# Two of the four weight sums of a seven-product pair, by accumulating DMAs from GpSimd

## The chip, the cores and the metric

One core of a Trainium2 chip runs the whole program. The metric is the device time of one execution in microseconds (us). The kernel before has a median of 1961.26 us in 3 runs (1959.46 to 1963.83).

## The reference

Two layers of a decoder trunk on 512 tokens of width 1024, with 16 learned tokens put in front (528 in all). Each layer has a gated feed-forward network, a mixer (pooling and gated linear attention side by side) and a second feed-forward network, each with a residual and a layer norm:

```python
def swiglu(x, w_gate, w_up, w_down):
    return (jax.nn.silu(x @ w_gate) * (x @ w_up)) @ w_down
...
    for l in range(DEPTH):
        h = layer_norm(a * h + 0.5 * swiglu(h, ffn1_w_gate[l], ffn1_w_up[l], ffn1_w_down[l]),
                       ln1_g[l], ln1_b[l])
        z = h @ w_in[l]
        ...
        h = layer_norm(a * h + y, ln2_g[l], ln2_b[l])
        h = layer_norm(a * h + 0.5 * swiglu(h, ffn2_w_gate[l], ffn2_w_up[l], ffn2_w_down[l]),
                       ln3_g[l], ln3_b[l])
    return h[:, N_META:]
```

All of it is float32, with d_ff = 2816, which is 22 tiles of 128. The change touches the gate and up products of the four feed-forward networks alone.

## The kernel before

**Precision.** A float32 operand is split into a high part (rounded to fp32r by ACT) and a low part (operand minus high part, by DVE or POOL). A product is three matmuls: high x high, high x low, low x high. So every weight block needs a `hi` and a `lo` before PE can use it.

**Stream of weights.** The weights lie in HBM as pieces of [128 x 1024] floats (512 KB), in the order of use. SP loads piece n into `raw[:, n % 2, :]` as soon as piece n-2 has been split (`wait_piece`, the loop at L314 to L316). ACT makes `w_hi` (`high_part`, L852), and POOL (`split`, L330) or, in the fast part, DVE (`raw_low`, L1195) makes `w_lo`, four slots of each.

**The fast part.** A network goes through the 22 tiles of d_ff in three phases of 8, 8 and 6. In a phase the gate and up pieces of each tile m come first, then 8 pieces of the down matrix. Tiles 0 to 3 are computed classically. For tiles 4 to 21 (18 in each network, 72 in all) the gate and up products together, taken over two halves of the tokens and two halves of the inner dimension, are a 2x2 block product. It is done with 7 block products in place of 8 (`fast_pair`, L430 and on): 7 x 4 x 3 = 84 matmuls of 128x264. Three of the seven use blocks of the weights as they lie in `raw`. Four use sums of weight blocks:

```python
s_sum[0] = u[low] + u[high]
s_sum[2] = g[low] + u[low]
s_sum[1] = s_sum[0] + g[low]
s_sum[3] = s_sum[1] + g[high]
```

where g and u are the gate and the up piece and low and high are their halves of 512 columns (`w_sums`, from L1172). ACT makes `s_hi` of each (`sum_high`, L846), DVE `s_lo` (`sum_low`, L1200). Sums of token blocks (`v_hi`, `v_lo`) are made once per network.

**The order of work** on every engine is written out by hand. While PE does pair i, DVE runs one iteration of the loop in `ffn` (L1237 to L1263): the four sums of pair i+1, `prod` of the tile before (L1129), `w_lo` of pair i+1 (L1195, twice), `s_lo` 1, `h_lo` (L1134), PS + `p_copy` (L1252), `s_lo` 2 and 3, PS + `u_copy` (L1259), `s_lo` 4. PE's last product of pair i needs the first of these two PSUM sums (`c22_done`). ACT does in the same time a copy of PSUM, `silu`, `w_hi` of the next pair, two copies, and the four `s_hi`. POOL does nothing in this part. It splits the classic pieces, the pieces of the down matrix and those of the mixer. At the end of a phase DVE adds the down product to X, piece by piece, and makes the sums of the next phase's first pair between pieces 4 and 5.

`s_lo_done`, `s_sum_done` and the like count instructions of one kind; 4*i+j stands for sum j of pair i.

## Time and profile before

| | us |
|---|---|
| median of 3 runs | 1961.26 |
| profiled execution, its own time | 1958.71 |
| its span | 1957.0 |
| PE matmul busy | 1886.8 |
| PE weight loads busy | 1802.3 |
| DVE busy | 1232.3 |
| ACT busy | 825.4 |
| POOL busy | 446.2 |

The busy time of an engine is the time in which at least one of its instructions ran. Matmuls overlap in the pipeline, so their mean durations (some 284 ns) are longer than the distance between two (some 121 ns). "Idle before" a group, with the releaser behind the arrow, tells what ended the waits of its instructions. The chain of work that ended last is 86% PE and 9% DVE.

### The profile page before, as it was taken

Reading aid. Unit: us, or ns where it says so; the run is one execution under the profiler, and the core shown is the slowest. Engines: PE = TensorE matmul, PEld = TensorE weight load, DVE = VectorE, ACT = ScalarE, POOL = GpSimd, SP = SyncE. Lnnn points to the kernel's source line nnn. Section 1 sums busy time; section 2 is a strip of 40 time slices with the busy share of each in tenths; the row PEclk is TensorE's granted clock in tenths of the full one; section 3 lists DMA queues with packets and bytes.
Section 4 is the critical chain, followed back from the end, with each engine's and each line's share of the span. In section 5 each row is a group of like instructions: output and inputs, shape, how many; then the busy total and the mean of one; then the engine's idle time right before and its main releaser. Section 6 shows DMA issues by size and latency. Waiting matters only on the chain.

```text
span 1957.0 us, 34609 instructions
## 1 busy us (share of the span) xinstructions
PE 1886.8 (96%) x14406; PEld 1802.3 (92%) x14406; DVE 1232.3 (63%) x1834; ACT 825.4 (42%) x1297; POOL 446.2 (23%) x200
## 2 busy tenths in 40 slices
PE   8999999989999999999999999999899999999996
PEld 8999999879898999999999999998797778899895
DVE  6728557667448837728487385577674488386475
ACT  4525435452125534525455254354431255345253
POOL 4030302332122240030521203023321221402113
PEclk9999999989898999999989999999898889999998
DMA  4333323321111332233323233232211113333232
GB/s 152 100 103 106 104 91 104 97 66 55 44 48 50 102 104 97 92 101 106 114 75 100 95 108 109 87 109 87 65 55 44 54 53 99 108 108 109 86 110 86
DMA packets 48828, 175.26 MB, mean 90 GB/s; under 512 B 5408, under 2 KB 5408, under 8 KB 48672
## 3 DMA queue, kind: packets, MB, share of 16 engines
q1 hardware_dynamic: 48240, 171.78, 28.0%
q8 instruction: 115, 1.88, 0.4%
q10 hardware_dynamic: 432, 1.25, 0.2%
q14 instruction: 41, 0.34, 0.1%
HBM read 170.92 MB, written 2.10 MB: 88 GB/s over the span
## 4 chain that ended last, share of the span: by engine, by line
PE 86%; DVE 9%; issue 2%; ACT 2%; DMA 1%; POOL 0%; DVEq 0%; ACTq 0%
PE PS L371 13%; PE PS L372 13%; PE PS L373 13%; PE PS L424 12%; PE PS L427 12%; PE PS L426 12%; PE PS L403 2%; PE PS L381 2%; PE PS L382 1%; PE PS L679 1%; PE PS L712 1%; DVE win L1533 1%; PE PS L524 1%; PE PS L710 1%; DVE qt L1488 1%
## 5 line engine op out<-in xcount | busy, mean ns | idle before, releaser
L330 POOL TENSOR_TENSOR w_lo<-raw,w_hi 128x1024 fp32r<-128x1024 f32 x172 | 431.3, 2511 | 1483.4 <-ACT w_hi L852 1058.8
L371 PE MATMUL PS<-h_hi,w_hi 128*128 128x264 f32 (+1 forms) x1238 | 370.2, 299 | 0.5 <-DVE h_lo L1134 0.2
L372 PE MATMUL PS<-h_lo,w_hi 128*128 128x264 f32 (+1 forms) x1238 | 369.7, 299 | 0.0
L373 PE MATMUL PS<-h_hi,w_lo 128*128 128x264 f32 (+1 forms) x1238 | 369.4, 298 | 0.0
L852 ACT ACTIVATE w_hi<-raw 128x1024 fp32r<-128x1024 f32 x240 | 215.1, 930 | 231.8 <-PE PS L373 179.1
L424 PE MATMUL PS<-v_hi,s_hi 128*128 128x264 f32 (+1 forms) x864 | 245.0, 284 | 6.1 <-DVE s_lo L1200 6.1
L371 PE MATMUL PS<-x_hi,w_hi 128*128 128x264 f32 (+2 forms) x796 | 245.2, 308 | 5.0 <-DVE ft L1526 4.9
L426 PE MATMUL PS<-v_lo,s_hi 128*128 128x264 f32 (+1 forms) x864 | 244.3, 283 | 0.0
L427 PE MATMUL PS<-v_hi,s_lo 128*128 128x264 f32 (+1 forms) x864 | 243.9, 282 | 0.0
L372 PE MATMUL PS<-x_lo,w_hi 128*128 128x264 f32 (+2 forms) x796 | 242.2, 304 | 0.0
L371 PEld LDWEIGHTS PS<-h_hi,w_hi 128*128 128x128 f32 x1238 | 233.0, 188 | 9.1 <-DVE h_lo L1134 1.6
L373 PE MATMUL PS<-x_hi,w_lo 128*128 128x264 f32 (+2 forms) x796 | 241.2, 303 | 0.0
L372 PEld LDWEIGHTS PS<-h_lo,w_hi 128*128 128x128 f32 x1238 | 233.1, 188 | 7.4
L373 PEld LDWEIGHTS PS<-h_hi,w_lo 128*128 128x128 f32 x1238 | 232.3, 188 | 7.3
L846 ACT ACTIVATE s_hi<-s_sum 128x512 fp32r<-128x512 f32 x288 | 177.5, 630 | 98.3 <-PE PS L427 96.8
L1200 DVE TENSOR_TENSOR s_lo<-s_sum,s_hi 128x512 fp32r<-128x512 f32 x288 | 190.1, 685 | 18.4 <-ACT s_hi L846 18.2
L424 PEld LDWEIGHTS PS<-v_hi,s_hi 128*128 128x128 f32 x864 | 162.5, 188 | 6.8 <-issue 6.8
L371 PEld LDWEIGHTS PS<-x_hi,w_hi 128*128 128x128 f32 x796 | 154.7, 194 | 12.9 <-issue 7.6
L427 PE MATMUL PS<-x_hi,w_lo 128*128 128x264 f32 (+1 forms) x576 | 163.0, 283 | 0.0
L426 PEld LDWEIGHTS PS<-v_lo,s_hi 128*128 128x128 f32 x864 | 162.9, 189 | 0.0
L424 PE MATMUL PS<-x_hi,w_hi 128*128 128x264 f32 (+1 forms) x576 | 162.7, 282 | 0.0
L427 PEld LDWEIGHTS PS<-v_hi,s_lo 128*128 128x128 f32 x864 | 162.4, 188 | 0.0
(217 smaller groups left out, 4008.2 us busy)
## 6 DMA issues: line engine op xcount, KB each, us to landing
raw<-in_stream SPq DMA_DIRECT2D x316, 512.0 KB, 3.7
raw_first<-in_stream SPq DMA_DIRECT2D x4, 512.0 KB, 5.7
out_t<-X SPq DMA_DIRECT2D x8, 256.0 KB, 2.1
X<-in_x_t SPq DMA_DIRECT2D x7, 264.0 KB, 7.5
par<-in_params ACTq DMA_DIRECT2D x2, 480.0 KB, 3.6
X<-in_x_t ACTq DMA_DIRECT2D x1, 264.0 KB, 4.5
```

The source lines that it names most:

```text
L330: nc.gpsimd.tensor_tensor(w_lo[:, slot, :], raw[:, slot % RAWS, :], w_hi[:, slot, :].bitcast(F32), ALU.subtract).then_inc(lo_done[slot], 1)
L371: nc.tensor.matmul(o, hi, rhs_hi[:, k, tok], start=first, stop=False)
L372: nc.tensor.matmul(o, hi, rhs_lo[:, k, tok], start=False, stop=False)
L373: return nc.tensor.matmul(o, lo, rhs_hi[:, k, tok], start=False, stop=last)
L381: nc.tensor.matmul(o, hi[j], x_hi[:, k, tok], start=k == 0, stop=False)
L403: m = nc.tensor.matmul(o, hi[j], x_lo[:, k, tok], start=False, stop=k == KC - 1)
L424: nc.tensor.matmul(o, hi[:, w], rhs_hi[:, k, :], start=start and k == 0, stop=False, skip_group_check=True)
L426: nc.tensor.matmul(o, hi[:, w], rhs_lo[:, k, :], start=False, stop=False, skip_group_check=True)
L427: m = nc.tensor.matmul(o, lo[:, w], rhs_hi[:, k, :], start=False, stop=stop and k == BAND - 1, skip_group_check=True)
L846: nc.scalar.activation(s_hi[:, j - 1, :], s_sum[:, j - 1, :], ACT.Copy).then_inc(S["s_hi_done"], 1)
L852: nc.scalar.activation(w_hi[:, n % SLOTS, part], raw[:, n % RAWS, part], ACT.Copy).then_inc(S["raw_hi"], 1)
L1200: V.tensor_tensor(s_lo[:, j - 1, :], s_sum[:, j - 1, :], s_hi[:, j - 1, :].bitcast(F32), ALU.subtract).then_inc(S["s_lo_done"], 1)
```

## The change

Two sums, 1 and 3, share the block u[low]. SP now loads this block twice into a new buffer `s_two` (one DMA with a broadcast source, 512 KB into two halves), double-buffered over pairs (`load_shared`). POOL waits for the landing and issues two accumulating DMAs of 256 KB each (`add_other`), which add u[high] to the one copy and g[low] to the other, straight from HBM. DVE keeps two adds, for sums 2 and 4, into a single buffer `s_more`. The up piece's load into `raw` brings only its upper half, as nothing else reads the lower one. ACT's and DVE's waits follow; at the first pair of a network they also wait for `v_lo`, because the new buffers share memory with `v_sum`. A first pair's DMAs stand two pieces earlier in the queues of SP and POOL.

```diff
--- before.py
+++ after.py
@@ -75,7 +75,6 @@
 BAND = 4
 BLOCK = BAND * P
 FAST = MT - CLASSIC
-S_ORDER = (1, 3, 2, 4)
 V_ORDER = (3, 1, 2, 4)
 
 
@@ -115,6 +114,13 @@
         if at <= r < at + 2 * nm:
             return m0 + (r - at) // 2 < CLASSIC
     return True
+
+
+FAST_GATES = {gate_piece(l, f, m) - 1: fast_index(l, f, m)
+              for l in range(DEPTH) for f in range(2) for m in range(CLASSIC, MT)}
+PHASE_FIRST = {fast_index(l, f, max(m0, CLASSIC)) for l in range(DEPTH) for f in range(2) for m0, _ in PHASES}
+
+SUMS_BEFORE = {max(n - 2, SLOTS + RAWS) if i in PHASE_FIRST else n: (i, n) for n, i in FAST_GATES.items()}
 
 
 def stream_ready(l, idx):
@@ -189,7 +195,7 @@
         warm = sb("warm", [P, 2])
         rms_eps = sb("rms_eps", [P, 1])
         with ExitStack() as s6:
-            s_sum = sb("s_sum", [P, 4, BLOCK], F32, s6)
+            s_two = sb("s_two", [P, 2, 2, BLOCK], F32, s6)
         acc_a = sb("acc_a", [P, HEADS, NCH, CH])
         acc_t = sb("acc_t", [META, HEADS, META])
 
@@ -207,6 +213,8 @@
         with ExitStack() as s5:
             s_hi = sb("s_hi", [P, 4, BLOCK], F32R, s5)
             s_lo = sb("s_lo", [P, 4, BLOCK], F32R, s5)
+            sb("reserve_v_sum", [P, 4 * BAND * HALF - 8 * BLOCK], F32, s5)
+            s_more = sb("s_more", [P, 2, BLOCK], F32, s5)
         with ExitStack() as s2:
             ex = sb("ex", [P, 4, T], F32, s2)
             kt = sb("kt", [P, 2, 2, T], F32, s2)
@@ -285,6 +293,8 @@
         x_loaded = [sem(f"x_loaded{k}") for k in range(KC)]
         first_full = [sem(f"first_full{i}") for i in range(SLOTS)]
         raw_full = [sem(f"raw_full{i}") for i in range(RAWS)]
+        s_loaded = [sem(f"s_loaded{i}") for i in range(2)]
+        s_added = [sem(f"s_added{i}") for i in range(2)]
         lo_done = [sem(f"lo_done{i}") for i in range(SLOTS)]
         block = ctx.enter_context(nc.Block())
 
@@ -296,6 +306,17 @@
 
         def wait_raw(eng, n):
             eng.wait_ge(raw_full[n % RAWS], 16 * ((n - SLOTS) // RAWS + 1))
+
+        def wait_added(eng, i):
+            eng.wait_ge(s_added[i % 2], 32 * (i // 2 + 1))
+
+        def two_term(i, j):
+
+            return s_two[:, i % 2, j // 2, :]
+
+        def summed_weights(i, j):
+
+            return two_term(i, j) if j % 2 else s_more[:, j // 2 - 1, :]
 
         def wait_stream(eng, l, idx):
             name, value = stream_ready(l, idx)
@@ -311,9 +332,23 @@
                     sp.dma_start(X[:, n, :], x_t[n * P:(n + 1) * P, :]).then_inc(x_loaded[n], 16)
             for n in range(RAWS):
                 sp.dma_start(raw[:, n, :], stream[SLOTS // RAWS, n]).then_inc(raw_full[n], 16)
+
+            def load_shared(i, gate):
+
+                if i > 0:
+                    sp.wait_ge(S["s_lo_done"], 4 * max(i - 1, 1))
+                if i % FAST < 2 and i >= FAST:
+                    sp.wait_ge(S["o_acc"], 4 * ((i // FAST + 1) // 2))
+                shared = stream[(gate + 1) // RAWS, (gate + 1) % RAWS][:, 0:BLOCK]
+                sp.dma_start(s_two[:, i % 2, :, :], shared.rearrange("p (o c) -> p o c", o=1)
+                             .to_broadcast([P, 2, BLOCK])).then_inc(s_loaded[i % 2], 16)
+
             for n in range(SLOTS + RAWS, DEPTH * LAYER_PIECES):
+                if n in SUMS_BEFORE:
+                    load_shared(*SUMS_BEFORE[n])
                 wait_piece(sp, n - RAWS)
-                sp.dma_start(raw[:, n % RAWS, :], stream[n // RAWS, n % RAWS]).then_inc(raw_full[n % RAWS], 16)
+                part = slice(BLOCK if n - 1 in FAST_GATES else 0, PIECE)
+                sp.dma_start(raw[:, n % RAWS, part], stream[n // RAWS, n % RAWS][:, part]).then_inc(raw_full[n % RAWS], 16)
 
             for k in range(KC):
                 sp.wait_ge(S["x_full_done"], DEPTH * LN_PER * KC - KC + k + 1)
@@ -352,7 +387,17 @@
                 n += 1
                 pool.wait_ge(S["consts"], n)
             nc.gpsimd.memset(acc_t[:, :, :], 0.0).then_inc(S["masks"], 1)
+
+            def add_other(i, gate):
+
+                pool.wait_ge(s_loaded[i % 2], 16 * (i // 2 + 1))
+                for j, n, part in ((1, gate + 1, slice(BLOCK, PIECE)), (3, gate, slice(0, BLOCK))):
+                    pool.dma_start(two_term(i, j), stream[n // RAWS, n % RAWS][:, part],
+                                   accum_op=ALU.add).then_inc(s_added[i % 2], 16)
+
             for n in range(SLOTS, DEPTH * LAYER_PIECES):
+                if n in SUMS_BEFORE:
+                    add_other(*SUMS_BEFORE[n])
                 if whole(n):
                     split(n)
             pool.wait_ge(S["mean_first_copied"], DEPTH * LN_PER)
@@ -840,10 +885,15 @@
 
             def sum_high(i, j):
 
-                act.wait_ge(S["s_sum_done"], 4 * i + S_ORDER.index(j) + 1)
+                if j % 2:
+                    wait_added(act, i)
+                else:
+                    act.wait_ge(S["s_sum_done"], 2 * i + j // 2)
                 if i > 0:
                     act.wait_ge(S[("p5_acc", "p6_acc", "p7_acc", "p3_acc")[j - 1]], i)
-                nc.scalar.activation(s_hi[:, j - 1, :], s_sum[:, j - 1, :], ACT.Copy).then_inc(S["s_hi_done"], 1)
+                if i % FAST == 0:
+                    act.wait_ge(S["v_lo_done"], 4 * (i // FAST) + 4)
+                nc.scalar.activation(s_hi[:, j - 1, :], summed_weights(i, j), ACT.Copy).then_inc(S["s_hi_done"], 1)
 
             def high_part(n, part):
 
@@ -1169,26 +1219,18 @@
                 V.tensor_tensor(v_lo[:, j - 1, :, 0:n], v_sum[:, j - 1, :, 0:n], v_hi[:, j - 1, :, 0:n].bitcast(F32),
                                 ALU.subtract).then_inc(S["v_lo_done"], 1)
 
-            def w_sums(i, gate, js):
-
-                low, high = slice(0, BLOCK), slice(BLOCK, 2 * BLOCK)
-                g, u = raw[:, gate % RAWS, :], raw[:, (gate + 1) % RAWS, :]
-                for j in js:
-                    if i > 0:
-                        dve.wait_ge(S["s_lo_done"], 4 * (i - 1) + j)
-                    if j == 1:
-                        wait_raw(dve, gate + 1)
-                        x = V.tensor_tensor(s_sum[:, 0, :], u[:, low], u[:, high], ALU.add)
-                    elif j == 3:
-                        wait_raw(dve, gate)
-                        x = V.tensor_tensor(s_sum[:, 2, :], g[:, low], u[:, low], ALU.add)
-                    elif j == 2:
-                        dve.wait_ge(S["s_sum_done"], 4 * i + 1)
-                        x = V.tensor_tensor(s_sum[:, 1, :], s_sum[:, 0, :], g[:, low], ALU.add)
-                    else:
-                        dve.wait_ge(S["s_sum_done"], 4 * i + 3)
-                        x = V.tensor_tensor(s_sum[:, 3, :], s_sum[:, 1, :], g[:, high], ALU.add)
-                    x.then_inc(S["s_sum_done"], 1)
+            def w_sums(i, gate):
+
+                g = raw[:, gate % RAWS, :]
+                wait_added(dve, i)
+                wait_raw(dve, gate)
+                if i > 0:
+                    dve.wait_ge(S["s_lo_done"], 4 * i)
+                if i % FAST == 0:
+                    dve.wait_ge(S["v_lo_done"], 4 * (i // FAST) + 4)
+                V.tensor_tensor(s_more[:, 0, :], two_term(i, 1), g[:, 0:BLOCK], ALU.add).then_inc(S["s_sum_done"], 1)
+                dve.wait_ge(S["s_sum_done"], 2 * i + 1)
+                V.tensor_tensor(s_more[:, 1, :], s_more[:, 0, :], g[:, BLOCK:PIECE], ALU.add).then_inc(S["s_sum_done"], 1)
 
             def raw_low(n, part):
                 dve.wait_ge(S["raw_hi"], n + 1)
@@ -1197,7 +1239,7 @@
 
             def sum_low(i, j):
                 dve.wait_ge(S["s_hi_done"], 4 * i + j)
-                V.tensor_tensor(s_lo[:, j - 1, :], s_sum[:, j - 1, :], s_hi[:, j - 1, :].bitcast(F32),
+                V.tensor_tensor(s_lo[:, j - 1, :], summed_weights(i, j), s_hi[:, j - 1, :].bitcast(F32),
                                 ALU.subtract).then_inc(S["s_lo_done"], 1)
 
             def pair_low(gate):
@@ -1228,7 +1270,7 @@
                                 v_low(l, f, span, 3)
                                 v_low(l, f, span, 4)
                             if m == CLASSIC - 2:
-                                w_sums(fast_index(l, f, CLASSIC), gate + 4, S_ORDER)
+                                w_sums(fast_index(l, f, CLASSIC), gate + 4)
                                 pair_low(gate + 4)
                             if m == CLASSIC - 1:
                                 for j in range(1, 5):
@@ -1239,7 +1281,7 @@
                         after_fast = m > m0 and m > CLASSIC
                         ps = 2 * (m % 2)
                         if follows:
-                            w_sums(i + 1, gate + 2, S_ORDER)
+                            w_sums(i + 1, gate + 2)
                         if after_fast:
                             fast_prod(l, f, m - 1, F22, span)
                         if follows:
@@ -1283,10 +1325,8 @@
                             dve.wait_ge(S["down_evac"], l * 32 + 16 * f + 8)
                             V.tensor_tensor(halves(X[:, mo, :], span), halves(X[:, mo, :], span), pair(mo % 4, span),
                                             ALU.add).then_inc(S["down_evac"], 1)
-                        if mo == 4:
-                            w_sums(i, nxt, S_ORDER[0:2])
-                        elif mo == 5:
-                            w_sums(i, nxt, S_ORDER[2:4])
+                        if mo == 5:
+                            w_sums(i, nxt)
                         elif mo == 6:
                             pair_low(nxt)
                             sum_low(i, 1)
```

On SP, before, every entry of the stream is one load of a piece that waits for the piece two before it (rows from the first pair's gate piece on; lo_done is the count of a slot's split pieces):

```order
L316 DMA raw<-in_stream 128x1024 [waits lo_done2]
L316 DMA raw<-in_stream 128x1024 [waits lo_done3]
L316 DMA raw<-in_stream 128x1024 [waits lo_done0]
L316 DMA raw<-in_stream 128x1024 [waits lo_done1]
L316 DMA raw<-in_stream 128x1024 [waits lo_done2]
```

Now, at the same place (again from the first pair's gate piece on), with `s_two` for the shared block:

```order
L351 DMA raw<-in_stream 128x1024 [waits lo_done2]
L351 DMA raw<-in_stream 128x512 [waits lo_done3]
L343 DMA s_two<-in_stream 128x2x512 [waits s_lo_done]
L351 DMA raw<-in_stream 128x1024 [waits lo_done0]
L351 DMA raw<-in_stream 128x512 [waits lo_done1]
L343 DMA s_two<-in_stream 128x2x512 [waits s_lo_done]
L351 DMA raw<-in_stream 128x1024 [waits lo_done2]
L351 DMA raw<-in_stream 128x512 [waits lo_done3]
L343 DMA s_two<-in_stream 128x2x512 [waits s_lo_done]
L351 DMA raw<-in_stream 128x1024 [waits lo_done0]
```

A load of `s_two` has come before each pair's gate piece, with a wait of its own on `s_lo_done`, and the up piece's load is half as wide.

On DVE, before, one steady iteration of the pair loop (names: PS is PSUM, p_copy and u_copy copies of it in SBUF):

```order
L1181 TENSOR_TENSOR s_sum<-raw 128x512
L1184 TENSOR_TENSOR s_sum<-raw 128x512
L1187 TENSOR_TENSOR s_sum<-s_sum,raw 128x512
L1190 TENSOR_TENSOR s_sum<-s_sum,raw 128x512
L1129 SCALAR_TENSOR_TENSOR prod<-PS,silu 128x528
L1195 TENSOR_TENSOR w_lo<-raw,w_hi 128x1024
L1195 TENSOR_TENSOR w_lo<-raw,w_hi 128x512
L1200 TENSOR_TENSOR s_lo<-s_sum,s_hi 128x512
L1134 TENSOR_TENSOR h_lo<-prod,h_hi 128x528
L1252 TENSOR_TENSOR PS<-PS,p_copy 128x264
L1200 TENSOR_TENSOR s_lo<-s_sum,s_hi 128x512 x2
L1259 TENSOR_TENSOR PS<-PS,u_copy 128x264
```

Now:

```order
L1231 TENSOR_TENSOR s_more<-s_two,raw 128x512
L1233 TENSOR_TENSOR s_more<-s_more,raw 128x512
L1179 SCALAR_TENSOR_TENSOR prod<-PS,silu 128x528
L1237 TENSOR_TENSOR w_lo<-raw,w_hi 128x1024
L1237 TENSOR_TENSOR w_lo<-raw,w_hi 128x512
L1242 TENSOR_TENSOR s_lo<-s_two,s_hi 128x512
L1184 TENSOR_TENSOR h_lo<-prod,h_hi 128x528
L1294 TENSOR_TENSOR PS<-PS,p_copy 128x264
L1242 TENSOR_TENSOR s_lo<-s_more,s_hi 128x512
L1242 TENSOR_TENSOR s_lo<-s_two,s_hi 128x512
L1301 TENSOR_TENSOR PS<-PS,u_copy 128x264
```

The adds that read `raw` alone are gone, and the two that are left follow each other.

On POOL, before, the whole program behind its constants:

```order
L350 AFFINE_SELECT level_mask<-level_mask 128x64
L354 MEMSET acc_t 16x64
L330 TENSOR_TENSOR w_lo<-raw,w_hi 128x1024 x172
L361 TENSOR_TENSOR X<-X,mean 128x512 x4
```

Now, from the first pieces on to the first down pieces:

```order
L365 TENSOR_TENSOR w_lo<-raw,w_hi 128x1024 [waits raw_hi] x2
L395 DMA s_two<-in_stream 128x512 [waits s_loaded0]
L395 DMA s_two<-in_stream 128x512
L365 TENSOR_TENSOR w_lo<-raw,w_hi 128x1024 [waits raw_hi] x2
L395 DMA s_two<-in_stream 128x512 [waits s_loaded1]
L395 DMA s_two<-in_stream 128x512
L395 DMA s_two<-in_stream 128x512 [waits s_loaded0]
L395 DMA s_two<-in_stream 128x512
L395 DMA s_two<-in_stream 128x512 [waits s_loaded1]
L395 DMA s_two<-in_stream 128x512
L365 TENSOR_TENSOR w_lo<-raw,w_hi 128x1024 [waits raw_hi] x6
```

Pairs of DMAs stand between the subtractions, each pair behind a wait for SP's load.

## Rows read from the trace of the kernel before

**Rows 1.** engines and granted clock, from the page

```profile
PE 1886.8 (96%) x14406; PEld 1802.3 (92%) x14406; DVE 1232.3 (63%) x1834; ACT 825.4 (42%) x1297; POOL 446.2 (23%) x200
...
PEclk9999999989898999999989999999898889999998
```

**Rows 2.** windows inside runs of pairs (us, busy (instructions) by engine, clock, DMA share, GB/s)

```profile
137.00:218.00 81.00, 81.00 (x671) 81.00 (x670) 66.78 (x105) 41.21 (x78) 0.00 (x0) 1.00 0.31 105
260.00:326.00 66.00, 66.00 (x547) 66.00 (x546) 50.63 (x79) 31.13 (x58) 0.00 (x0) 1.00 0.29 97
...
744.00:825.00 81.00, 81.00 (x670) 81.00 (x669) 66.63 (x104) 40.03 (x75) 0.00 (x0) 1.00 0.31 105
```

**Rows 3.** the page's group of PE matmuls with summed weights

```profile
L424 PE MATMUL PS<-v_hi,s_hi 128*128 128x264 f32 (+1 forms) x864 | 245.0, 284 | 6.1 <-DVE s_lo L1200 6.1
```

**Rows 4.** timeline of PE, first pair of the first network (start us, us, engine)

```profile
59.00 0.28 PE L427 MATMUL PS<-x_hi,w_lo 128*128 128x264 f32 x1
60.81 0.36 PE L424 MATMUL PS<-v_hi,s_hi 128*128 128x264 f32 x1 [1.52 <-DVE s_lo L1200]
```

**Rows 5.** timeline of DVE, the same place

```profile
57.93 0.71 DVE L1129 SCALAR_TENSOR_TENSOR prod<-PS,silu 128x528 f32<-128x528 f32 x1 [2.24 <-issue]
59.35 0.71 DVE L1134 TENSOR_TENSOR h_lo<-prod,h_hi 128x528 fp32r<-128x528 f32 x1 [0.71 <-ACT h_hi L834]
59.97 2.49 DVE L1200 TENSOR_TENSOR s_lo<-s_sum,s_hi 128x512 fp32r<-128x512 f32 x4
```

**Rows 6.** timeline of ACT, the same place

```profile
58.67 0.65 ACT L834 ACTIVATE h_hi<-prod 128x528 fp32r<-128x528 f32 x1 [5.98 <-DVE prod L1129]
59.22 2.17 ACT L846 ACTIVATE s_hi<-s_sum 128x512 fp32r<-128x512 f32 x4
```

**Rows 7.** timeline of DVE, a steady iteration in the third phase

```profile
302.32 0.44 DVE L1252 TENSOR_TENSOR PS<-PS,p_copy 128x264 f32<-128x264 f32 x1 [0.37 <-PE PS L427]
...
305.11 0.68 DVE L1181 TENSOR_TENSOR s_sum<-raw 128x512 f32<-128x512 f32 x1
...
307.11 0.69 DVE L1190 TENSOR_TENSOR s_sum<-s_sum,raw 128x512 f32<-128x512 f32 x1
307.71 0.70 DVE L1129 SCALAR_TENSOR_TENSOR prod<-PS,silu 128x528 f32<-128x528 f32 x1
308.56 1.83 DVE L1195 TENSOR_TENSOR w_lo<-raw,w_hi 128x1024 fp32r<-128x1024 f32 x2 [0.15 <-ACT w_hi L852]
310.83 0.69 DVE L1200 TENSOR_TENSOR s_lo<-s_sum,s_hi 128x512 fp32r<-128x512 f32 x1 [0.44 <-ACT s_hi L846]
...
312.50 0.44 DVE L1252 TENSOR_TENSOR PS<-PS,p_copy 128x264 f32<-128x264 f32 x1 [0.36 <-PE PS L427]
...
314.69 0.69 DVE L1200 TENSOR_TENSOR s_lo<-s_sum,s_hi 128x512 fp32r<-128x512 f32 x1 [0.20 <-ACT s_hi L846]
316.20 0.69 DVE L1181 TENSOR_TENSOR s_sum<-raw 128x512 f32<-128x512 f32 x1 [0.82 <-DMA raw<-in_stream]
```

**Rows 8.** timeline of PE, its first matmul after PS+p_copy

```profile
313.77 0.28 PE L424 MATMUL PS<-v_hi,w_hi 128*128 128x264 f32 x1
```

**Rows 9.** DMA queue and issues (packets, MB, share; KB each, us to landing)

```profile
q1 hardware_dynamic: 48240, 171.78, 28.0%
...
raw<-in_stream SPq DMA_DIRECT2D x316, 512.0 KB, 3.7
...
out_t<-X SPq DMA_DIRECT2D x8, 256.0 KB, 2.1
```

**Rows 10.** timeline of SP, one issue of a raw load

```profile
309.82 0.33 SPq L316 DMA_DIRECT2D raw<-in_stream  x1
```

**Rows 11.** timeline of POOL, a subtraction of a down piece

```profile
101.01 2.40 POOL L330 TENSOR_TENSOR w_lo<-raw,w_hi 128x1024 fp32r<-128x1024 f32 x1 [2.23 <-ACT w_hi L852]
```

**Rows 12.** DVE's first sum, groups by line (busy us, mean ns, idle before)

```profile
L1181 DVE TENSOR_TENSOR s_sum<-raw 128x512 f32<-128x512 f32 x72 | 49.6, 690 | 34.6 <-DMA raw<-in_stream 34.2
```

**Rows 13.** POOL's subtraction, the page's groups

```profile
L330 POOL TENSOR_TENSOR w_lo<-raw,w_hi 128x1024 fp32r<-128x1024 f32 x172 | 431.3, 2511 | 1483.4 <-ACT w_hi L852 1058.8
```

**Rows 14.** timeline of DVE, h_lo beside the subtraction of rows 11

```profile
101.83 2.14 DVE L1134 TENSOR_TENSOR h_lo<-prod,h_hi 128x528 fp32r<-128x528 f32 x1 [0.71 <-ACT h_hi L834]
```


## The prediction

> **What bounds the kernel now.** The page's engine line comes first: PE is busy 1886.8 of 1957.0 us, DVE 1232.3 us, and the granted clock is full almost throughout [rows 1]. PE is the suspect, but "busy" is an average, so the stretches that the change touches are read next. In windows that lie inside runs of seven-product pairs PE is busy 81.00 of 81.00, 66.00 of 66.00 and 81.00 of 81.00 us at a clock of 1.00, the upper level (2.4 GHz), with DVE at 66.78, 50.63 and 66.63 us [rows 2]. DVE is heavily loaded there, but nobody on PE waits for it. The group of PE's matmuls that could wait for a weight sum stands idle 6.1 us in the whole run [rows 3], and that is all that PE loses to s_lo.
>
> Where these 6.1 us lie is seen at the first pair of a feed-forward network (there are four, so about 1.5 us each; [rows 4] has one of 1.52 us). The chain into it is DVE prod of the last classic tile at 57.93, ACT h_hi at 58.67, ACT s_hi from 59.22, DVE s_lo from 59.97 [rows 5, 6]. DVE stood idle 2.24 us before that prod: the four sums of this pair had long been made. This wait is the h_hi that is queued ahead of s_hi on ACT, and the change does not touch it.
>
> One steady iteration on DVE [rows 7] starts its sums at 305.11, and the last s_lo runs from 314.69 to 315.38, which is 10.27 us. The period, from one PS+p_copy to the next, is 312.50-302.32 = 10.18 us. In it DVE waits 0.15 us for ACT's w_hi, 0.44 us and 0.20 us for ACT's s_hi, and 0.36 us for PE: 1.15 us of slack, small but there. The PS+p_copy ends at 312.94 and PE needs it at 313.77 [rows 8]: another 0.83 us.
>
> **The change, part by part.**
> 1. Two adds leave DVE: the four sums take 305.11 to 307.71, 2.60 us; the two that stay take at most 0.69+0.69 = 1.38 us. Saved: 1.22 us on each of 72 pairs, 88 us of DVE. What it is worth is zero: PE has no wait there to give back [rows 2]. Even DVE gets little of it in time, since the next instruction, prod, needs a silu from ACT and w_lo then waits for w_hi (0.15 us already now). The cover of the cost side grows: slack 1.15+1.22 = 2.4 us per iteration.
> 2. The stream of bytes. Before, a pair loads 2 x 512 KB. Packet time: 28.0% of 16 engines' 1957 us over 48240 packets [rows 9] is 0.18 us for a packet of mostly 4 KB, 8 packets per engine for 512 KB, so 1.45 us of an engine. After: gate piece 1.45, upper half of the up piece 0.73, the doubled shared block 16 packets of 2 KB, 1.46, and two accumulating DMAs with 16 packets of 2 KB. An accumulating packet is not in the trace: at least a plain 2 KB one (0.09 us), and at most three such, since it reads two sides and writes one (0.27 us); I take two (0.18 us), because reading the two sides can overlap writing. Sum 5.1 to 8.0 us of an engine per 10.18 us: the engines don't become the bound at either end. Cost zero.
> 3. The new chain of waits, which is the real question. SP issues the shared load for pair i+3 only when the last s_lo of pair i+1 is done, the end of the iteration of pair i. It must land; POOL then issues two DMAs; both must land; and DVE asks for them at the start of the iteration of pair i+2. That is one period, 10.18 us, after the issue. Call the chain C. Shared load: 3.7 us to landing for 512 KB [rows 9]. POOL's two issues: bounded below by SP's 0.33 us each [rows 10], above by a POOL instruction of 2.4 us [rows 11]; I take 1.0 each, nearer to SP's since it is the same act. Fixed part of a landing: 3.7-1.45 = 2.25 us. The packets behind it: 8 x 0.18 = 1.45 us (the first DMA's lie under the second's issue). The gate and upper-half loads fall into the same stretch, 4.7 us after the iteration starts (309.82 against 305.11, [rows 7, 10]), with 1.45+0.73 = 2.2 us of engine; I count half, 1.1. C = 3.7+2.0+2.25+1.45+1.1 = 10.5 us. The low end is 3.7+2.1 = 5.8 us, with a 256 KB store as the nearest row; the high end is 3.7+4.8+2.25+16x0.27+2.2 = 17.3 us.
>  When does C decide? DVE's own iteration from the sums to the last s_lo without waits is D = 10.27-1.15-1.22 = 7.9 us. Issue to ask takes C, ask to the next issue of that slot takes D, and two buffers alternate, so the period is (C+D)/2 if that exceeds PE's 10.18: C above 12.5 us. My 10.5 is 2 us below it: DVE waits about 0.3 us per iteration for the adds, and PE does not notice. Cost zero.
>  The Trainium skill (DMA: Bandwidth & Descriptors, "Anatomy of one DMA — SWDGE (gpsimd) path") gives some 2.0 us plus the bytes at 436 GB/s for a DMA from GpSimd, 2.6 us for 256 KB; by it C would be nearer 8 us. [...]
> 4. Raw loads. DVE's first sum waited 34.2 us in all for them [rows 12] ([rows 7] has one of 0.82). The up piece's lower half is no longer asked for there, so this wait shrinks or turns into one for the adds. Worth zero for the same reason as 1.
> 5. Queues passed. SP: the gate load stands behind the shared load, whose condition (end of an iteration) comes about 4 us before the gate load's own (w_lo). POOL: its w_lo subtractions exist only outside the pairs; two adds slip ahead of the last two of a phase and ahead of two at each network's start, 2 us at most by my price, 4.8 by the bound. POOL waits 2.23 us for ACT before such a w_lo [rows 11] and 1483 us in all [rows 13], and the pieces it makes are used more than one piece later. Zero.
>
> Sum: the profiled execution has 1957.0 us of span and 1958.71 us of its own time; terms add to 0. It stands 2.5 us below the median of 1961.26, so the forecast is the median, **1961.3 us**.
>
> **The rivals.**
> *A, slower: the chain through two queues is longer than 12.5 us.* For it: an accumulating packet has no row here, POOL's issue neither, and the high end 17.3 gives a period of 12.6 us. Against: my middle. The third and later pairs of each phase are ruled by it: (2+6+4) x 4 = 48. At C = 14 the period is 10.95, +0.77 x 48 = +37 us, about 1998; at 17.3 it is +2.4 x 48 = +116, 2077. Its signs would be DVE's first add waiting long for s_two in every iteration and PE falling below full busy in the windows.
> *B, slower: POOL's work on descriptors holds up DVE.* Under a POOL subtraction at 101.01-103.4 [rows 11] the h_lo, 0.71 us elsewhere [rows 5], took 2.14 [rows 14]: DVE instructions do get stretched when POOL works. If each of the two DMAs does that once, 2 x 1.43 = 2.9 us against 2.4 of slack: a DVE-bound period of 10.18+0.5, +24 us over 48 pairs, 1985.
>  The Trainium skill (SBUF — State Buffer, "Who interferes with whom") holds that a DVE instruction with two SBUF inputs conflicts with GpSimd instructions that read SBUF, not with ones that only write it; by that rule B would not happen, and the sum stays. The trace agrees for the reading kind alone.
> *C, faster: the four waits of PE at the first pairs go.* 6.1 us in all, so 1955. Against: DVE idle 2.24 us just there.
>
> **How the numbers follow.** A measurement of this kernel can tell about 0.2%, 3.9 us. Forecast (hidden) 0.57, A 0.25, B 0.10, C 0.08. Of C only the full 6.1 us counts as faster: 0.06, and the rest goes to same. A and B may come out small (C near 12.6): some 0.02 of them stay within 0.2%. That gives faster 0.06, same 0.61, slower 0.33. The range starts at 1957 (run to run spread and part of C) and reaches to 2000, A at a chain of 14 us and all of B; beyond lies A with dear packets, about 0.12. The likeliest case alone: 1958 to 1965.
>
> **What would show it.** Right: DVE busy falls by some 88 us to about 1145; PE's busy share inside the windows stays at 1.00; period 10.2 us; the chain of waits keeps its shares; q1 and a new POOL queue carry about 1.75 times the bytes within the pairs. Step 3 is read from SP's issue of s_two, its landing, and the start of DVE's first add two iterations on: 10.5 us expected, with a wait of a few tenths. Wrong: PE idle before a seven-product matmul, released by DVE's p_copy sum or s_lo, with DVE waiting for s_two (A), or DVE's subtractions of 0.69 us stretched to 2 while POOL issues (B). A gate load that lands later than about 5 us after its issue would show step 2 priced too low.

## The result, and the profile after

| | before | after |
|---|---|---|
| median of 4 runs, us | 1960.99 | 1988.55 |
| lowest to highest, us | 1959.46 to 1963.83 | 1987.0 to 1989.93 |
| profiled execution: its time; span, us | 1958.71; 1957.0 | 1987.0; 1985.3 |
| PE busy; not busy, us | 1886.8; 70.2 | 1896.3; 89.0 |
| DVE busy, us | 1232.3 | 1141.0 |

The change makes the kernel slower: the ratio is 1.0139, with a 95% interval of 1.0121 to 1.0156. That is 27.6 us. The forecast was 1961.3 us. The time lies in the predicted range only because the range reached to 2000 us for rival A. The 28.3 us of span are 18.8 us in which PE stands and 9.5 us in which it is busy for longer.

From the page of the changed kernel, beside [rows 1, 3, 9]: engines and clock, the two data queues (packets, MB, share of 16 engines), the chain that ended last, POOL's DMAs, PE's matmuls with summed weights, and the DMA issues (KB each, median us to landing).

```profile
PE 1896.3 (96%) x14406; PEld 1806.8 (91%) x14406; DVE 1141.0 (57%) x1690; ACT 827.8 (42%) x1297; POOL 568.4 (29%) x344
...
PEclk9899999999999999999999999998897989999998
...
q1 hardware_dynamic: 67824, 190.66, 30.3%
q0 software_dynamic: 20736, 37.76, 12.0%
...
PE 65%; DVE 15%; DMA 13%; issue 4%; ACT 2%; POOL 1%; DVEq 0%; ACTq 0%
...
L395 POOL DMA_DIRECT2D s_two<-in_stream x144 | 125.3, 1015 | 564.5 <-DMA s_two<-in_stream 558.2
...
L469 PE MATMUL PS<-v_hi,s_hi 128*128 128x264 f32 (+1 forms) x864 | 246.3, 285 | 12.0 <-DVE s_lo L1242 6.1
...
raw<-in_stream SPq DMA_DIRECT2D x244, 512.0 KB, 3.7
s_two<-in_stream SPq DMA_DIRECT2D x72, 512.0 KB, 4.7
s_two<-in_stream POOLq DMA_DIRECT2D x144, 256.0 KB, 5.9
raw<-in_stream SPq DMA_DIRECT2D x72, 256.0 KB, 5.7
```

The DMAs of s_two now stand on the chain that ended last. DVE is 91 us less busy, about as forecast, and nothing of it shows in the time. The page counts a DMA instruction of POOL as busy time, so POOL's rise from 446.2 to 568.4 us is mostly those 144 instructions (125.3 us).

Windows, the first two at the first pairs of the kernel, the others inside runs of pairs (us, busy (instructions) of PE, PEld, DVE, ACT and POOL, clock, DMA share, GB/s). [Rows 2] had PE busy for all of its windows.

```profile
59.00:72.00 13.00, 6.26 (x50) 5.87 (x49) 3.82 (x6) 4.79 (x10) 1.76 (x2) 0.94 0.51 156
72.00:80.00 8.00, 6.09 (x28) 5.91 (x29) 4.77 (x8) 2.75 (x6) 1.73 (x2) 0.66 0.82 142
165.00:240.00 75.00, 74.53 (x611) 73.98 (x611) 50.00 (x81) 41.40 (x77) 14.85 (x14) 1.00 0.63 158
764.00:842.00 78.00, 76.58 (x628) 76.03 (x627) 52.69 (x84) 43.62 (x81) 13.80 (x14) 1.00 0.59 156
1745.00:1823.00 78.00, 73.78 (x616) 72.31 (x615) 51.06 (x83) 42.43 (x80) 12.94 (x14) 1.00 0.60 156
```

So there are two losses: a heavy one once, at 59 to 80 us, and a light one in the pairs, 0.5 of 75 us in one place and 4.2 of 78 us in the last network. Measured as the stretches of seven-product matmuls (from the start of the first to the start of the last, for each of the twelve phases, worked out from both traces), the kernel loses 32.3 us in them: 11.5 in the very first (42.36 to 53.88 us), 12.5 in the three of the last network (178.5 to 190.9) and 8.3 in the other eight. Some 4 us come back outside.

**The first loss.** SP, DVE and PE at the second pair of the first network, from three timelines of the changed kernel:

```profile
63.88 0.38 SPq L343 DMA_DIRECT2D s_two<-in_stream  x1
64.30 0.94 SPq L351 DMA_DIRECT2D raw<-in_stream  x2
```

```profile
63.16 0.69 DVE L1242 TENSOR_TENSOR s_lo<-s_more,s_hi 128x512 fp32r<-128x512 f32 x1
75.20 0.69 DVE L1231 TENSOR_TENSOR s_more<-s_two,raw 128x512 f32<-128x512 f32 x1 [11.35 <-DMA s_two<-in_stream]
```

```profile
72.11 0.59 PE L469 MATMUL PS<-v_hi,s_hi 128*128 128x264 f32 x1 [5.33 <-ACT u_copy L948]
...
79.45 0.36 PE L469 MATMUL PS<-v_hi,w_hi 128*128 128x264 f32 x1 [1.80 <-DVE PS L1294]
```

The shared load of pair 1 leaves at 63.88, right behind the last s_lo of pair 0, which ends at 63.16+0.69 = 63.85. It need not wait for it: pair 1 has the other buffer, which holds nothing that is still needed. But the condition reads `4 * max(i - 1, 1)`, and for i = 1 that is the same 4 as for i = 2. The gate and up loads of pair 1 are queued behind it on SP and leave at 64.30 too, though their slots were free: without that wait they leave at 54.88 (e1 below). DVE then waits 11.35 us and PE stands for 5.33 and 1.80 us. During the first stand the clock falls: a window from 66.8 to 70.5 us, inside the stand, has 1.00, one from 70.6 to 77.3 has 0.50. The window from 72 to 80 us above has 0.66 of full, a mixture of the two levels (1.2 and 2.4 GHz). The last section counts at most 4.4 us for that, so the standing and the clock together (5.33+1.80+4.4 = 11.5 us) account for what the first stretch lost. Where the other 5 us of longer "busy" lie I did not follow up.

**The second loss.** One chain in the second phase, issue by issue (SP, POOL, DVE):

```profile
190.28 0.38 SPq L343 DMA_DIRECT2D s_two<-in_stream  x1
```

```profile
196.29 1.73 POOL L395 DMA_DIRECT2D s_two<-in_stream  x2 [9.36 <-DMA s_two<-in_stream]
```

```profile
204.11 0.69 DVE L1231 TENSOR_TENSOR s_more<-s_two,raw 128x512 f32<-128x512 f32 x1 [3.12 <-DMA s_two<-in_stream]
```

From SP's issue to DVE's add it takes 13.83 us, where I had 10.5. Over the 48 pairs that the rule governs, issue to landing of the last add is 12.92 us in the mean (10.4 to 15.2): 4.82 for the shared load, 0.28 until POOL issues, 0.57 until its second issue, 7.25 until that has landed. Since this is longer than one period, the chains overlap: when SP issues a shared load, the adds of the pair before travel for another 2.8 us (mean). In the waits (us in all, times, longest):

```profile
DVE s_more L1231 <- DMA s_two<-in_stream: 133.2, 41, 11.3
...
DVE s_more L1231 <- DMA raw<-in_stream: 19.2, 7, 3.4
...
PE PS L469 <- DVE PS L1294: 13.1, 19, 2.7
```

PE's wait is for DVE's sum into PS, which is queued behind the adds on DVE: the sign named for rival A.

### The profile page after: what moved, and what is told of

Its sections match the earlier page's. It is cut to its first block, busy times and chain, and to the rows that moved or that the text cites. A ratio compares the mean times of both kernels' runs of the same rounds, so it can differ in the third digit from the quotient of the medians.

```text
span 1985.3 us, 34482 instructions
## 1 busy us (share of the span) xinstructions
PE 1896.3 (96%) x14406; PEld 1806.8 (91%) x14406; DVE 1141.0 (57%) x1690; ACT 827.8 (42%) x1297; POOL 568.4 (29%) x344
## 3 DMA queue, kind: packets, MB, share of 16 engines
q0 software_dynamic: 20736, 37.76, 12.0%
## 4 chain that ended last, share of the span: by engine, by line
PE 65%; DVE 15%; DMA 13%; issue 4%; ACT 2%; POOL 1%; DVEq 0%; ACTq 0%
PE PS L416 13%; PE PS L417 12%; PE PS L418 12%; DMA s_two<-in_stream 12%; PE PS L469 6%; PE PS L472 6%; PE PS L471 6%; DVE s_lo L1242 2%; DVE w_lo L1237 2%; PE PS L448 2%; PE PS L426 2%; PE PS L427 1%; DMA raw<-in_stream 1%; DVE h_lo L1184 1%; DVE prod L1179 1%
## 5 line engine op out<-in xcount | busy, mean ns | idle before, releaser
L395 POOL DMA_DIRECT2D s_two<-in_stream x144 | 125.3, 1015 | 564.5 <-DMA s_two<-in_stream 558.2
L469 PEld LDWEIGHTS PS<-v_hi,s_hi 128*128 128x128 f32 x864 | 163.2, 189 | 13.5 <-issue 6.8
L471 PE MATMUL PS<-x_lo,w_hi 128*128 128x264 f32 (+1 forms) x576 | 162.3, 282 | 0.0
```

The lines of the kernel that those rows point to most:

```text
L395: pool.dma_start(two_term(i, j), stream[n // RAWS, n % RAWS][:, part], accum_op=ALU.add).then_inc(s_added[i % 2], 16)
L469: nc.tensor.matmul(o, hi[:, w], rhs_hi[:, k, :], start=start and k == 0, stop=False, skip_group_check=True)
L471: nc.tensor.matmul(o, hi[:, w], rhs_lo[:, k, :], start=False, stop=False, skip_group_check=True)
```

## The experiments

All ratios are to the kernel before on the same chip, with the 95% interval. Theory T1 is the two separate losses above. T2 says that the added traffic delays the loads of the weights themselves. T3 puts the cost on the fixed part of a GpSimd DMA.

**e1: the needless wait taken away.**

```diff
-                if i > 0:
-                    sp.wait_ge(S["s_lo_done"], 4 * max(i - 1, 1))
+                if i > 1:
+                    sp.wait_ge(S["s_lo_done"], 4 * (i - 1))
```

> Undoes one wait alone: the shared load of pair 1 no longer waits for the last s_lo of pair 0 (its buffer is unused by then). Theory T1 (two separate losses: 11.5 us in the first phase from this one wait, some 21 us in the other eleven phases from the chain of shared load, two accumulating DMAs and DVE): the first phase falls from 53.9 us to about 43, the total to 1977 to 1979, the other phases stay. Rival (the first phase lost its time to the traffic at the start, not to this wait): under 3 us gained.

Measured: 1980.2 us (1972.03 to 1982.94), ratio 1.0102 [1.0078, 1.0127]. In the trace the gate and up loads of pair 1 leave at 54.88, DVE's longest wait for s_two falls from 11.3 to 3.8 us, and the first stretch is 42.84 us again:

```profile
54.88 0.93 SPq L351 DMA_DIRECT2D raw<-in_stream  x2
```

```profile
DVE s_more L1231 <- DMA s_two<-in_stream: 119.9, 42, 3.8
```

The first loss is shown: 8.4 us by the medians (7.4 us when each is taken against the kernel before on its own chip), 11.0 us by the stretch. The median is just above the expected 1977 to 1979. The profiled execution was the fastest of the four (1972.03 us) and 8 us under their median, so its stretches understate what e1 usually loses. The rest of the waiting (119.9 us on DVE) stays, so the second loss is another thing.

**e2: the same, and the shared load released one s_lo earlier,** when the buffer's last reader of the pair is done.

```diff
-                    sp.wait_ge(S["s_lo_done"], 4 * max(i - 1, 1))
+                    sp.wait_ge(S["s_lo_done"], 4 * (i - 2) + 3)
```

> As the first, and the shared load waits for three of the four s_lo of the pair two before (the first and third read s_two, the fourth does not), which is some 1.9 us earlier in each iteration. T1 (the chain of about 12.9 us is over the 12.5 us that two buffers allow): PE's stalls in the pairs go, total 1961 to 1965. Rival T2 (the added traffic delays the gate and up loads, and that is what PE waits for): the total stays at 1972 or more, since the traffic is the same.

Measured: 1975.35 us, 1.0082 [1.0057, 1.0107]. T1's 1961 to 1965 did not come; the total is where rival T2 had it, and only e4 below decides against T2. The issue is earlier by 1.0 us, the time between the ends of the third and the fourth s_lo in the trace (I had expected 1.9), but the chain became longer by 1.2 us: 13.79 us in the mean against e1's 12.57. The shared load now takes 5.2 us to land (e1: 4.6) and the adds 6.1 (5.9), and DVE waits longer for its own raw load:

```profile
s_two<-in_stream SPq DMA_DIRECT2D x72, 512.0 KB, 5.2
s_two<-in_stream POOLq DMA_DIRECT2D x144, 256.0 KB, 6.1
```

```profile
DVE s_more L1231 <- DMA s_two<-in_stream: 97.7, 31, 4.7
DVE s_more L1231 <- DMA raw<-in_stream: 48.7, 17, 3.6
```

What the earlier issue wins, the longer chain takes back: over the 48 pairs the adds land 2.9 us after DVE could ask for them, and 2.8 us in e1. The intervals of e1 and e2 overlap; whether e2 is better is not settled.

**e3: plain copies in the place of the accumulating ones** (first wait as in the change). The kernel leaves out the additions of sums 1 and 3.

```diff
-                                   accum_op=ALU.add).then_inc(s_added[i % 2], 16)
+                                   ).then_inc(s_added[i % 2], 16)
```

> The two DMAs from GpSimd copy in place of accumulating, so sums 1 and 3 are wrong; same bytes, queues and waits as the changed kernel. T1: a 2 KB packet falls from 178 to about 84 ns, 16 of them save 1.5 us of the chain, 12.9 to 11.4 us, under the limit; only the first phase still loses: 1972 to 1976. Rival T3 (the fixed part of a GpSimd DMA makes the chain long, not the accumulation): under 4 us gained, 1985 or more.

Measured: 1972.49 us, 1.0066 [1.0044, 1.0087]. The first stretch still has its loss (50.46 us), and after it every stretch is the one of before, but for 1.9 us in the last network. These stretches are from the profiled execution, at 1967.46 us the fastest of four. The chain is 9.80 us where 11.4 were expected, 5.00 of it from the second copy's issue to its landing. POOL's page rows and the queue:

```profile
q0 software_dynamic: 11520, 37.76, 6.1%
...
L395 POOL DMA_DIRECT2D s_two<-in_stream x144 | 77.7, 543 | 574.1 <-DMA s_two<-in_stream 571.2
...
s_two<-in_stream SPq DMA_DIRECT2D x72, 512.0 KB, 3.9
s_two<-in_stream POOLq DMA_DIRECT2D x144, 256.0 KB, 4.3
```

The same bytes through the same queue cost 6.1% of the engines in place of 12.0%, and half of the time on POOL's sequencer. A DMA from POOL as such (T3) is not the price; the accumulating is, with the smaller packets that come with it (last section).

**e4: all the traffic, none of the waiting.** DVE makes two sums from the gate piece in `raw` alone, and all four s_hi and s_lo read these two (so it does two adds less than the kernel before and leaves the up piece out of all four sums); the DMAs all run, and nobody reads what they make.

```diff
-            return two_term(i, j) if j % 2 else s_more[:, j // 2 - 1, :]
+            return s_more[:, j // 2 - 1 if j % 2 == 0 else j // 2, :]
...
-                    sp.wait_ge(S["s_lo_done"], 4 * max(i - 1, 1))
+                    wait_added(sp, i - 2)
...
-                wait_added(dve, i)
...
-                V.tensor_tensor(s_more[:, 0, :], two_term(i, 1), g[:, 0:BLOCK], ALU.add).then_inc(S["s_sum_done"], 1)
+                V.tensor_tensor(s_more[:, 0, :], g[:, BLOCK:PIECE], g[:, 0:BLOCK], ALU.add).then_inc(S["s_sum_done"], 1)
```

> All DMAs of the change run, but nobody reads s_two: DVE makes two adds from raw, all four s_hi and s_lo read these two, so the sums are wrong. SP reuses a buffer once its adds have landed. T1: without the waits on s_two the traffic costs nothing on PE, 1960 to 1964, as before the change. T2: the loads into raw come late, and 10 us or more of the loss stay.

Measured: 1958.7 us, 0.9997 [0.9987, 1.0008]. The queue is as busy as in the change, the shared load even takes 6.8 us to land, and PE is busy for all of a window inside the pairs:

```profile
q0 software_dynamic: 20736, 37.76, 12.2%
...
s_two<-in_stream SPq DMA_DIRECT2D x72, 512.0 KB, 6.8
```

```profile
750.00:830.00 80.00, 80.00 (x662) 80.00 (x661) 59.20 (x90) 42.48 (x79) 10.91 (x13) 1.00 0.61 162
```

T2 is refuted: traffic at 0.61 of the engines costs nothing where nobody waits for the chain. DVE does wait for its raw loads (40.3 us in all, against 34.2 before), and PE does not notice. The run says a second thing: with two adds less on DVE and no chain at all, the time is that of before. So the most that this change could have won is too small to measure.

**e6: a third buffer for s_two,** in memory that the feed-forward network does not otherwise use then. T1' says that the chain matters only against the period that the buffers grant; T4 says that the DMA engines are too slow for any number.

```diff
-                if i > 0:
-                    sp.wait_ge(S["s_lo_done"], 4 * max(i - 1, 1))
+                if i > 2:
+                    sp.wait_ge(S["s_lo_done"], 4 * (i - 2))
```

> The changed kernel with three buffers of s_two in place of two (the needless wait of pair 1 is gone with it); traffic, packets and instructions are the same. T1' (the loss is the chain of 13 us against the period that two buffers grant): the shared load goes out one iteration earlier, DVE's first add never waits for s_two, all twelve phases are back at 42.4, 81.4 and 61.0 us (78.5 and 58.8 in the last network), total 0.999 to 1.001 of before. Rival T4 (the 16 DMA engines are too slow for accumulation beside the loads, so any number of buffers ends in a stall): at least 8 us of loss stay.

Measured: 1964.4 us, 1.0024 [1.0013, 1.0036]. Five sixths of the loss are gone, T4 falls, and 4.6 us stay, against T1's 0.999 to 1.001. T1' also had DVE never waiting for the adds, and it waits 58.0 us for them (30.4+27.6). The landings, and DVE's waits:

```profile
s_two<-in_stream SPq DMA_DIRECT2D x48, 512.0 KB, 6.3
...
s_third<-in_stream SPq DMA_DIRECT2D x24, 512.0 KB, 7.4
```

```profile
DVE s_more L1239 <- DMA raw<-in_stream: 34.2, 23, 3.3
DVE s_more L1239 <- DMA s_two<-in_stream: 30.4, 15, 4.2
DVE s_more L1239 <- DMA s_third<-in_stream: 27.6, 11, 4.0
```

The chain is now 15.72 us in the mean, longer than ever. Released early, the shared load (the second row of SP's timeline) leaves right behind 768 KB of raw loads (the first), where it used to leave some 4 us after them:

```profile
183.63 0.93 SPq L359 DMA_DIRECT2D raw<-in_stream  x2
184.61 0.51 SPq L351 DMA_DIRECT2D s_two<-in_stream  x1
```

This order also says why the third buffer grants less than it seems to. A shared load stands in SP's queue behind the raw loads of the pair before it, and leaves 5.9 us (median of the 48 pairs) after its own condition is met. From its issue to DVE's asking are 14.1 us in the mean, against 10.0 in the change: 4 us more, and not a whole period of 10.18. The chain of 15.72 us is longer than that too. The stretches of matmuls lose most in the last network (181.9 against 178.5 us). How much of the chain's length is that order on SP and how much the accumulating packets, these runs do not separate.

**e8: one accumulating DMA in place of two.** DMA makes sum 1; DVE adds g[low] to the second copy itself, three adds in all. First wait as in e1.

```diff
-                for j, n, part in ((1, gate + 1, slice(BLOCK, PIECE)), (3, gate, slice(0, BLOCK))):
+                for j, n, part in ((1, gate + 1, slice(BLOCK, PIECE)),):
...
+                V.tensor_tensor(two_term(i, 3), two_term(i, 3), g[:, 0:BLOCK], ALU.add).then_inc(S["s_sum_done"], 1)
```

> Two buffers, without pair 1's wait, and one accumulating DMA in place of two: DVE adds g[low] to the second copy itself. 8 packets of 178 ns and one issue less shorten the chain by about 2 us, 12.6 to 10.6 us. T1': below the limit of 12.5 us, no stall in the pairs, 0.999 to 1.002 of before. If a stall of 5 us or more stays, the limit lies lower than the prediction had it, or the chain is not what decides.

Measured: 1959.98 us, 1.0003 [0.9993, 1.0012]. The time is as T1' had it; the chain is 9.43 us, shorter than the expected 10.6: the shared load, too, lands sooner (3.83 us in the mean, 4.63 in e1):

```profile
s_two<-in_stream POOLq DMA_DIRECT2D x72, 256.0 KB, 5.2
```

```profile
DVE s_two L1231 <- DMA s_two<-in_stream: 16.9, 13, 2.5
```

**e5: on the kernel before, the four s_hi of the first pair ahead of the last classic tile's h_hi on ACT, and the four s_lo ahead of its prod on DVE.** This asks for the 6.1 us of [rows 3].

```diff
+                            if m == CLASSIC - 1:
+                                for j in range(1, 5):
+                                    sum_high(fast_index(l, f, CLASSIC), j)
                             h_high(m, m0, F22, span)
...
+                            if m == CLASSIC - 1:
+                                for j in range(1, 5):
+                                    sum_low(fast_index(l, f, CLASSIC), j)
                             dve.wait_ge(S["silu_done"], F22 + (m + 1))
```

> The kernel before the change, with the four s_hi and s_lo of each network's first pair made ahead of h_hi and prod of the last classic tile, on ACT and on DVE. It tests why PE stands idle 1.52 to 1.68 us at the four first pairs: if the cause is the h_hi that is queued ahead of s_hi (as the prediction says), the four waits vanish and the total falls by 6 to 7 us, to 0.9965 of the time before. Rival: the new order delays prod by 0.2 us or more each and some of it comes back, under 3 us gained.

Measured: 1954.38 us, 0.9969 [0.9955, 0.9983], faster than both kernels. The run moves two orders at once. [Rows 5] show h_lo, which waits for h_hi, ahead of s_lo on DVE as well, so by these rows an early s_hi on ACT alone would have left s_lo where it was. An early s_lo on DVE alone could not run at all, since its s_hi would be queued behind an h_hi that needs prod. The page's group of [rows 3], and DVE where [rows 5] had prod at 57.93 and s_lo at 59.97:

```profile
L424 PE MATMUL PS<-v_hi,s_hi 128*128 128x264 f32 (+1 forms) x864 | 244.9, 283 | 0.1
```

```profile
56.33 2.49 DVE L1200 TENSOR_TENSOR s_lo<-s_sum,s_hi 128x512 fp32r<-128x512 f32 x4
58.74 0.70 DVE L1129 SCALAR_TENSOR_TENSOR prod<-PS,silu 128x528 f32<-128x528 f32 x1
```

**e7 and e9: the early order of e5 put on e6 and on e8** (the same lines moved).

> Three buffers and the early s_hi and s_lo of the first pairs together. If both causes are right the two add up: 0.9965 of before, as the early order alone. If it comes out faster than the early order alone by over 2 us, the two adds less on DVE have a worth that the prediction put at zero.

> One accumulating DMA as in e8_one_accumulate, and the early s_hi and s_lo of the first pairs as in e5_early_first_lo. The chain takes 9.4 us there, 3 us under the limit, so it should not eat the gain of the early order as the two-DMA chain did with three buffers (1.0015 in place of 0.9969). Expected 0.996 to 0.998 of before, the same as the early order alone, since one add less on DVE is worth nothing. If it ends at 0.999 or more, a first pair that starts earlier meets a chain that is still too long there.

Measured: e7 1962.46 us, 1.0015 [1.0001, 1.0028], not the expected 0.9965; e9 1954.73 us, 0.9968 [0.9956, 0.998], as expected. In e7 the first pair does start earlier, but at the second or third pair of each network PE then waits behind the adds, by 0.3 to 2.1 us at a time, and the four first phases are 7.4 us longer than before: the early order asks the long chain for its result sooner. With the chain of 9.4 us there is room for it. e9 and e5 are equal: one add less on DVE is worth nothing also there.

## Why the prediction was wrong, step by step

The forecast of 1961.3 us was 27 us too low, and its likeliest case, a chain that costs nothing, did not happen: step 3 made the chain 2.4 us too short, and step 5 missed the first wait. That the time lies in the range is partly luck. Rival A's own arithmetic gives +11 us at the measured chain of 12.92 us (0.23 us on 48 pairs), about 1972 us; what brings the time to 1988.55 is the first pair, which no rival had, and a last network that lost more than A's single limit allows.

**What bounds the kernel** held. PE has no wait in the pairs that a lighter DVE could give back; e4 takes the two adds away at no price at all and gets 0.9997.

**Step 1** held: DVE busy fell by 91 us (88 forecast), worth 0.

**Step 2** held in its conclusion. Its sign of error did not show for the gate loads (4.4 us to landing, median of the 72), though the upper halves of the up pieces took 5.7. The middle price of an accumulating packet, 0.18 us, is the one measured: the median over the trace is 178 ns, against 84 ns for a plain packet of 2 KB on the queue of SP. The engines are no bound, which e4 shows.

**Step 3, the sum of the chain, is the step that failed.** Its rule, that a chain above a limit costs time, was right, and its terms were too small: 12.9 us against 10.5. The shared load took 4.8, not 3.7, since it travels beside other transfers: the adds of the pair before are under way for its first 2.8 us, while in e3 and e8, where they have landed within 0.2 us of its issue, it took 3.9 and 3.8. The two issues of POOL were well priced (1015 ns each), but the second follows the first by 0.57 us, so the first DMA's eight 2 KB packets on every engine (1.4 us) do not lie under it, as I had put it. Nearly all 16 are behind the second issue: 12.0% of 1985.3 us over 144 DMAs is 1.65 us of every engine for each, 3.3 us for both, where I counted 8 x 0.18 = 1.45. The rest is the weight loads of the same stretch, which I had counted by half; the runs do not part them from the wait for a first packet. The last 7.25 us of the chain were 1.0+2.25+1.45+1.1 = 5.8 us in my sum. So 1.1 us were missing in the shared load and 1.45 in the adds, against 0.15 us too many between the two issues.

By my formula a chain of 12.92 us and D = 7.9 us give a period of 10.41, 0.23 us above 10.18: 8.3 us over the 36 pairs of the first three networks, and 8.3 is what their eight later stretches lost. That it agrees so well is luck. The mean over the first three networks alone is 12.79 us, and those stretches hold 34 of the pairs: 5.6 us. For e1's trace, with 12.57 us, the formula gives 2 us where these stretches lost 5.9. The chains scatter by 5 us, and a mean hides that. For the last network the formula needs another limit, and I gave it the same one: its pairs take 78.45/8 = 9.8 us, so the chain may be only 2 x 9.8-7.9 = 11.7 us long there. With the mean of 13.30 us there the formula gives 0.8 us on 12 pairs, 9.6 us, and 12.5 were measured. So it says where the cost begins and not how large it is. With two buffers, the traces with chains of 9.4 and 9.8 us (e8, e3) lose at most 2 us in the stretches behind the first, and those with 12.6 us and more (e1, e2, the change) lose 12 to 21. The limit lies between them, as the formula has it (for e2, whose load leaves 1.0 us earlier, it would be 13.5, and the chain was 13.79). How the loss grows above it can't be told from these, as single executions of e1 and e2 differ by 11 and 13 us.

The Trainium skill (DMA: Bandwidth & Descriptors, "Anatomy of one DMA — SWDGE (gpsimd) path") has a fit from which I estimated 2.6 us for a GpSimd DMA of 256 KB. These runs have 5.9 us for the accumulating one, 5.2 with one alone per pair (e8), and 4.3 for plain copies (e3), all beside other traffic; no run has one on an idle chip.

**Step 4** held: DVE's wait for raw fell from 34.2 to 19.2 us.

**Step 5 failed for SP.** I wrote that the gate load stands behind the shared load, whose condition comes about 4 us before the gate load's own. That is so for steady pairs. For the second pair of the kernel the gate load's own condition had been met long before, and `max(i - 1, 1)` set it behind an s_lo that it has nothing to do with. This needed no rare row: the diff has the value for i = 1, and the queue's own condition in the same iteration. POOL's queue held: its subtractions wait for ACT as before.

**Rival A** was the right mechanism for the second loss, at a chance of 0.25. Its price, 37 us at C = 14, was for a chain 1 us longer than the one that came, and it did not have the 11 us of the first pair. **Rival B** did not happen: the subtractions of DVE keep their duration beside POOL's issues.

```profile
L1242 DVE TENSOR_TENSOR s_lo<-s_two,s_hi 128x512 fp32r<-128x512 f32 x144 | 98.6, 685 | 4.4 <-ACT s_hi L896 4.4
...
L1231 DVE TENSOR_TENSOR s_more<-s_two,raw 128x512 f32<-128x512 f32 x72 | 49.8, 691 | 153.9 <-DMA s_two<-in_stream 133.2 <-DMA raw<-in_stream 19.2
```

These are the groups of DVE by line, to be read against the 0.69 us of [rows 7] and the 690 ns of [rows 12]. Here the rule of the Trainium skill (SBUF — State Buffer, "Who interferes with whom") and the trace agree: the DMAs that POOL issues leave DVE alone.

**Rival C** did not come, since the change leaves the order at the first pairs alone: PE still waits 6.1 us for s_lo there. e5 takes this wait away by changing the order on ACT and on DVE. I had named h_hi ahead of s_hi on ACT alone; h_lo ahead of s_lo on DVE [rows 5] holds s_lo back as well.

## What to carry to other kernels

Before work is moved off an engine, ask what its whole removal would win; e4's kind of run, which leaves the work out and keeps the rest, answered it: nothing. Work moved into a chain of transfers through two queues has to fit into the time from its first issue to the consumer's asking. That is at most (number of buffers x period) less the consumer's own part, and less where the first issue stands in a queue behind loads that are released later (14.1 us with three buffers in e6, where the formula has 22.6). The chain is to be summed with every packet behind the last issue and every neighbour's transfer counted in full, and compared for the shortest period that occurs. And evaluate a written-out wait for the first two or three indices by hand: an in-order queue makes everything behind it pay.

## What the runs showed that was not expected

- An accumulating DMA of 2 KB rows moved packets of 2 KB at 178 ns; the same DMA without accumulating moved mostly 4 KB packets (11520 in place of 20736) at half of the share, and its instruction on POOL took 543 in place of 1015 ns (e3).
- Releasing a load earlier made its chain 1.2 us longer (e2) or 2.8 us (e6, against the change), because it fell among other transfers.
- In a stand of PE of 5.33 us the granted clock fell, and in the windows of the next 13 us it had means of 0.50 to 0.76. Windows of the changed kernel; in the kernel before, and in e1 without the needless wait, the same stretch had 1.00:

```profile
72.00:75.00 3.00, 2.89 (x13) 2.89 (x14) 0.00 (x0) 0.34 (x2) 1.73 (x2) 0.50 0.85 129
75.00:80.00 5.00, 3.20 (x17) 3.02 (x17) 4.77 (x8) 2.41 (x4) 0.00 (x0) 0.76 0.81 149
80.00:82.00 2.00, 2.00 (x14) 2.00 (x13) 1.87 (x4) 0.00 (x0) 0.00 (x0) 0.70 0.70 270
82.00:85.00 3.00, 3.00 (x18) 3.00 (x18) 1.02 (x3) 0.99 (x3) 0.00 (x0) 0.63 0.51 174
85.00:88.00 3.00, 3.00 (x27) 3.00 (x27) 2.47 (x3) 2.29 (x5) 1.73 (x2) 1.00 0.26 23
```

The clock alone cost at most 3.0x0.50+5.0x0.24+2.0x0.30+3.0x0.37 = 4.4 us there, of the 11.5 us that the stretch lost. This wait on PE cost more than itself.
